# Pool sums moved from GpSimd to VectorE, one logarithm behind the last exponential, and the first gate matmuls between the last attention units of a fused decoder layer

## What is computed

```python
h = rms_norm(x, g_pre_mix); proj = h @ w_in            # q, k, v, u, gates
for window, dilation in ((128, 1), (512, 4), (2048, 16)):
    o_g, lse_g = dilated_window_attention(rope(q_g), rope(k_g), v_g)
o_attn = sum_g softmax_g(lse_g) * o_g                  # 4 heads x 64
y_pool = (trailing mean of u over 2/4/8/16 - u) @ w_pool_mix * pool_scale
merged = sigmoid(gate_a) * (o_attn @ w_proj_attn) + sigmoid(gate_p) * (y_pool @ w_proj_pool)
x = x + rms_norm(merged @ w_out, g_post_mix)
x = x + rms_norm(swiglu(rms_norm(x)) @ w_down)
```

## Time and profile before

| | us |
|---|---|
| runs | 996.31, 996.59, 1165.07; median 996.59 |
| profiled execution | 1000.57 |
| its span on the slowest core (core 7) | 999.0 |
| spans of the other cores | 989.2 to 997.9 |
| PE, DVE, ACT, POOL busy in the span | 926.5, 394.0, 350.3, 320.1 |
| attention stage on core 7 | 212.9 to 318.0 |

### The profile page before, as it was taken

How to read it: one execution, slowest core, us unless ns; L and a number is a source line. 1 busy time by engine, 2 the same in 40 slices (tenths; PEclk the granted TensorE clock), 3 DMA queues, 4 the chain that set the end, 5 groups by cost and what they waited for, 6 DMA issues and landing times.

```text
span 999.0 us, 15229 instructions; the slowest of 8 cores (989.2 to 999.0 us)
## 1 busy us (share of the span) xinstructions
PE 926.5 (93%) x5532; PEld 462.5 (46%) x5532; DVE 394.0 (39%) x552; ACT 350.3 (35%) x603; POOL 320.1 (32%) x318
## 2 busy tenths in 40 slices
PE   1779899998897999999998999999999999999993
PEld 1455454466664444444454444444444444444441
DVE  2576785558876233323677121111112111211111
ACT  4763763369776222224662111110111111111101
POOL 3446587733400433233565111111322000001231
PEclk9999999999998999999999999999999999999997
DMA  8799310000230452114979666664234444430332
GB/s 225 235 231 257 87 47 22 1 2 2 35 53 8 80 84 43 22 22 90 314 252 184 115 110 117 115 108 87 92 127 114 76 85 66 82 64 1 127 110 80
DMA packets 32874, 99.16 MB, mean 99 GB/s; under 512 B 4256, under 2 KB 4256, under 8 KB 32800
## 3 DMA queue, kind: packets, MB, share of 16 engines
q0 software_dynamic: 15296, 42.05, 25.7%
q1 hardware_dynamic: 17360, 56.11, 16.9%
q10 hardware_dynamic: 144, 0.03, 0.0%
HBM read 123.43 MB, written 16.78 MB: 140 GB/s over the span
## 4 chain that ended last, share of the span: by engine, by line
PE 80%; DMA 6%; ACT 4%; issue 4%; DVE 3%; POOL 2%; SPq 1%; DVEq 0%; ACTq 0%; POOLq 0%
PE ps L1229 15%; PE ps L1195 15%; PE ps L1198 15%; PE ps L449 10%; PE ps L969 6%; PE ps L972 6%; PE ps L538 5%; DMA xst<-xh 2%; DMA xin<-xo 2%; DMA xst<-xo 2%; PE ps L979 1%; PE ps L976 1%; PE ps L826 1%; PE ps L804 1%; POOL x1b L1045 1%
## 5 line engine op out<-in xcount | busy, mean ns | idle before, releaser
L1195 PE MATMUL ps<-hT,wgu 128*128 128x512 bf16 x672 | 158.7, 379 | 0.0
L1198 PE MATMUL ps<-hT,wgu 128*128 128x512 bf16 x672 | 158.7, 379 | 0.0
L1229 PE MATMUL ps<-wdn,ffT 128*128 128x512 bf16 x704 | 152.3, 379 | 1.5 <-DMA wdn<-wdn 1.5
L1210 DVE TENSOR_TENSOR ffT<-ps,sa 128x512 bf16<-128x512 f32 x88 | 60.8, 691 | 222.5 <-PE ps L1198 222.5
L1209 ACT ACTIVATE sa<-ps 128x512 f32<-128x512 f32 x88 | 52.7, 598 | 241.5 <-PE ps L1195 241.5
L1229 PEld LDWEIGHTS ps<-wdn,ffT 128*128 128x128 bf16 x704 | 68.8, 98 | 84.7 <-issue 1.9
L1198 PEld LDWEIGHTS ps<-hT,wgu 128*128 128x128 bf16 x672 | 65.7, 98 | 79.3
L1195 PEld LDWEIGHTS ps<-hT,wgu 128*128 128x128 bf16 x672 | 65.6, 98 | 78.6
L74 POOL DMA_DIRECT2D wgu<-wgu x42 | 22.5, 537 | 236.1 <-PE ps L1198 227.5
L449 PE MATMUL ps<-hT,wqk 128*128 128x512 bf16 x384 | 91.6, 383 | 0.6 <-DVE hT L432 0.6
L1045 POOL TENSOR_TENSOR x1b<-tb,xin 128x1024 f32<-128x1024 f32 x31 | 72.8, 2350 | 55.7 <-DVE tb L1040 29.9
(11 more groups left out here) (131 smaller groups left out, 1175.7 us busy)
## 6 DMA issues: line engine op xcount, KB each, us to landing
wgu<-wgu POOLq DMA_DIRECT2D x42, 512.0 KB, 6.3
xst<-xh SPq DMA_DIRECT2D x16, 512.0 KB, 16.7
xin<-xo SPq DMA_DIRECT2D x16, 512.0 KB, 5.4
x1s<-x1b SPq DMA_DIRECT2D x16, 512.0 KB, 3.7
xin<-x1s SPq DMA_DIRECT2D x16, 512.0 KB, 4.3
out<-x1b SPq DMA_DIRECT2D x15, 512.0 KB, 2.9
xst<-xo SPq DMA_DIRECT2D x12, 512.0 KB, 10.8
wdn<-wdn POOLq DMA_DIRECT2D x22, 256.0 KB, 7.3
```

The lines of the kernel that those rows point to most:

```text
L1195: e1 = pe.op(lambda e, k=k, wbuf=wbuf, ba=ba, tok=tok: e.matmul(ps[:, ba, :], lhsT=wbuf[:, 0, k, :], rhs=hT[:, k, tok], start=(k == 0), st ...
L1198: e2 = pe.op(lambda e, k=k, wbuf=wbuf, bb=bb, tok=tok: e.matmul(ps[:, bb, :], lhsT=wbuf[:, 1, k, :], rhs=hT[:, k, tok], start=(k == 0), st ...
L1210: ef = dve.op(lambda e, ub=ub, bb=bb, j=j, b=b: e.tensor_tensor(out=ffT[:, j, b * 512:(b + 1) * 512], in0=ps[:, bb, :], in1=sa[ub][:, :], ...
L1229: ev = pe.op(lambda e, j=j, h2=h2, pr_=pr_, il=il: e.matmul(ps[:, pr_[0] + h2, :], lhsT=ffT[:, j, il * 128:(il + 1) * 128], rhs=wdn[:, j, ...
```

## The change

It does four things. The adds of the second pool half run on DVE, in place of POOL, one in each of iterations 9 to 12, 17, 20, 23 and 26, with their means in 13, 14, 33 and 35; what depends on them moves too, the mapping to iterations 37 to 40 and the weight loads to 36. `norm_inv(2)` moves from iteration 46 to 47, behind the exponential of unit 47, and `norm_mul(2)` from 48 to 49. The 16 gate matmuls of the first merge unit are issued in iterations 45 to 49, ahead of the apply of that iteration, into banks 6 and 7, and the merge's bank sets become (6, 7, 0, 1) and (2, 3, 4, 5). The copy of unit 0 names its wait for the rotary stage itself.

```diff
-            ev2 = act.op(lambda e: e.activation(out=dst, in_=src, func=AF.Copy), waits=[ev])
+            ev2 = act.op(lambda e: e.activation(out=dst, in_=src, func=AF.Copy), waits=[ev] + (ev_rope if u == 0 else []))
...
-    h10, h11 = window_half(pool, 1, 0), window_half(pool, 1, 1)
+    h10, h11 = window_half(dve, 1, 0), window_half(dve, 1, 1)
+    c1_steps = dict(zip((9, 10, 11, 12, 13, 14, 17, 20, 23, 26, 33, 35), h10[0] + h10[1] + h11[0] + h11[1]))
...
+    def gate_mm():
+        n = len(ev_gate)
+        h, k, bank = n // 8, n % 8, 6 + n // 8
+        if k == 0:
+            pe.wait(bank_free[bank], wg_ev[0])
+        ev_gate.append(pe.op(lambda e: e.matmul(ps[:, bank, :], lhsT=wgs[0][:, h, k, :], rhs=hT[:, k, 0:512], start=(k == 0), stop=(k == 7)), signal=(k == 7)))
...
-        if 25 <= u < 29:
-            pool_mix(1, u - 25)
+        if u in c1_steps:
+            c1_steps[u]()
+        if 37 <= u < 41:
+            pool_mix(1, u - 37)
             ev_yp = act.last()
+        for _ in range({45: 3, 46: 3, 47: 3, 48: 4, 49: 3}.get(u, 0)):
+            gate_mm()
...
-        if u == 29:
+        if u == 36:
...
-        if u >= 38 and u % 4 == 2 and u < 50:
+        if u in (38, 42, 47):
             norm_inv((u - 38) // 4)
-        if u >= 40 and u % 4 == 0:
+        if u in (40, 44, 49):
             norm_mul((u - 40) // 4)
...
-    mring = Ring([(0, 1, 2, 3), (4, 5, 6, 7)])
+    mring = Ring([(6, 7, 0, 1), (2, 3, 4, 5)])
...
+            if mu == 1:
+                e1, e2 = ev_gate[7], ev_gate[15]
+            else:
```

More of the change, by code:

```diff
@@ L884, in build_program @@
     napp = 0
+    ev_gate = []
+    def gate_mm():
[4 more added lines that the diff above has]
+        ev_gate.append(pe.op(lambda e: e.matmul(ps[:, bank, :], lhsT=wgs[0][:, h, k, :], rhs=hT[:, k, 0:512], start=(k == 0), stop=(k == 7)), signal=(k == 7)))
     for u in range(-1, len(units) + 2):
@@ L899, in build_program @@
                 ev_z0.append(dve.last())
-                for f in h10[0]:
-                    f()
         if 12 <= u < 16:
             pool_mix(0, u - 12)
[L904 to L910, removed]
-        if 25 <= u < 29:
-            pool_mix(1, u - 25)
+        if u in c1_steps:
+            c1_steps[u]()
+        if 37 <= u < 41:
+            pool_mix(1, u - 37)
             ev_yp = act.last()
+        for _ in range({45: 3, 46: 3, 47: 3, 48: 4, 49: 3}.get(u, 0)):
+            gate_mm()
         if napp <= u - 2:
@@ L967, in build_program @@
             pe.wait(frm, bank_free[b1], bank_free[b2], bank_free[b3], bank_free[b4], ev_wg, ev_wp, ev_yp)
[L968 to L973, removed]
+            if mu == 1:
+                e1, e2 = ev_gate[7], ev_gate[15]
+            else:
+                for k in range(8):
+                    e1 = pe.op(lambda e, k=k, wb=wb, b1=b1, tok=tok: e.matmul(ps[:, b1, :], lhsT=wgs[wb][:, 0, k, :], rhs=hT[:, k, tok], start=(k == 0), stop=(k == 7)),
+                               signal=(k == 7))
+                for k in range(8):
+                    e2 = pe.op(lambda e, k=k, wb=wb, b2=b2, tok=tok: e.matmul(ps[:, b2, :], lhsT=wgs[wb][:, 1, k, :], rhs=hT[:, k, tok], start=(k == 0), stop=(k == 7)),
+                               signal=(k == 7))
             pe.wait(ev_oT[b])
```

## The result

The changed kernel takes 989.27 us (median of 6 runs, 988.52 to 990.98), beside 996.85 for the kernel before (median of 6). The ratio is 0.9927, 95% interval 0.9914 to 0.9941: 7.6 us in the median, under 1% and clearly more than nothing. The forecast was 989.6. The profiled execution took 988.52 us, where the forecast for it was 993.6; its slowest core (core 3) has a span of 987.0, the others 982.7 to 986.6.

The account below looks back on a forecast made before the run. TensorE was taken as the bound, with 14 idle microseconds in attention and slow matmuls around its end. 2.5 - 1.3 + 5.8 = 7.0 us won: 993.6 from the profiled 1000.57, 989.6 from the median 996.59; range 985.5 to 995.5.

Parts of the forecast that it names:

- First part: Attention stage, pool adds moved from POOL to DVE: 3.3 us of waits go, 0.8 come, 2.5 us won.
- allowed lateness: Units 17 to 26: spread adds may make DVE 1.7 us late before an apply waits; only the last two overstep.
- Second part: Pool maps and loads moved later: V block of unit 40 waits behind norm_inv(0) on ACT, 1.3 us lost.
- The weight loads are issued in unit 36 instead of 29.: Attention stage: loads land 9.0 us after issue, needed 17 us later; nothing lost, the 1.4 us V-block stop left.
- Third part, apply 47: Attention's end: norm_inv(2) behind exp 47 brings apply 47 to 315.0 instead of 316.99, 2.0 us won.
- Third part, apply 47 to the third merge unit: Merge start: 11.15 us becomes 7.35, 3.8 won with a new 1.4 us wait, half clock counted as gone.
- A microsecond won ahead of it should be a microsecond at the end.: Behind 318 us everything hangs on TensorE's own order, so attention-stage gains should reach the end whole.
- Rival 1: Clock falls anyway between units 45 and 49: 3.4 us of the gain lost, 993.0 us; chance 0.12.
- the early stretch: 235 to 248 us: clock stayed at 1.00 with TensorE busy 9.87 of 13.00 us, held against clock loss in gaps.
- Rival 2: DVE becomes the bound of units 17 to 35: 3.3 us lost instead of 0.8, 992.1 us; chance 0.12.
- Rival 3: Unit 40's 1.3 us stop lowers the clock until the merge: 7 us slower, 1003.6 us; chance 0.03.
- Rival 4: DVE and ACT hold the tail, apply 47 stays in place: 2.0 us less gain, 991.6 us; chance 0.10.

Follow-up runs that it names:

- gates back: Changed kernel with the 16 gate matmuls back behind the last apply, in the first merge unit: 993.06 us, ratio 0.9939 to the kernel before.
- sums back on POOL: Changed kernel with the second pool half's adds back on POOL and, with their means, at their old places: 993.40 us, ratio 0.9941 to the kernel before.
- logarithm at 47: Kernel before with only norm_inv(2) moved to iteration 47 and norm_mul(2) to 49: 996.92 us, ratio 0.9975 to the kernel before.
- no sums: Kernel before without the four POOL adds of the second pool half's second token half, means reading old sums: 999.67 us, timed once or twice.
- all three edits: Changed kernel with first logarithms at 40 and 43, second-token-half adds every fourth unit, last logarithm behind first merge sigmoids: 989.19 us; with banks renamed too, 988.97.
- logarithms at 40 and 43: Changed kernel with norm_inv(0) in iteration 40, norm_mul(0) in 42 and norm_inv(1) in 43: 991.99 us, timed once or twice.
- late loads: Kernel before with gate and mapping weight loads written in iteration 36, waiting for VectorE's last instruction there: 998.78 us, timed once or twice.

## Why the prediction was right

The stretch from the scores to the projection took 244.77 us on core 7 before and takes 237.86 on core 3 now, 6.9 us for the 7.0 of the sum. But that agreement is partly luck: two things that the prediction did not see, each of about 1.4 us, cancel on core 7 (a stop behind the weight loads that went away, and the projection that starts late). On the profiled execution the forecast missed: 993.6 against 988.52.

- **First part (2.5 expected).** Right in mechanism and size: 3.3 us of waits go and 1.0 comes (0.8 expected), 2.0 to 2.3 when taken back. The waits follow the second, third and fourth add, not only the last two: allowed lateness was put too high. The prediction gave the 3.3 to masks and means together; 2.3 of it goes when POOL's adds alone are left out.
- **Second part (1.3 lost).** The wait is 1.29 us, at the V block named. "1.3 us lost" was still too large as a term: removing it gains 0.35, since 0.9 comes back as waits of applies 44 and 45. The step that failed treats the terms of the second and third part as independent.
- **"The weight loads are issued in unit 36 instead of 29."** Wrong about the present: POOL's list is not tied to the loop on PE. The loads left when the mean they wait for was done, at 266.35 in the kernel before and at 287.01 now. And the stop that I "leave as it is" was tied to them: 0.2 to 1.4 us won on four cores.
- **Third part, apply 47 (2.0 expected).** Right: 2.2 with the logarithm alone on undisturbed cores, of which the gates in the gaps, which the sum took as free, cost up to 0.5 (99.26 against 98.74). From the scores to apply 47 the undisturbed cores go from 102.6 to 99.26, 3.3 us for 2.5 - 1.3 + 2.0 = 3.2.
- **Third part, apply 47 to the third merge unit (3.8 expected).** 318.35 - 310.74 = 7.61 us for 7.35, so 3.5 won, with a wait of 1.54 for 1.4. The clock stayed at 1.00, as counted.
- **"A microsecond won ahead of it should be a microsecond at the end."** This failed. From the third unit's gates to the projection it was 457.64 - 328.14 = 129.50 us and is 449.40 - 318.35 = 131.05. The new order of the bank sets costs 1.40 of the 1.55 at the other end of the merge, on all eight cores; I had read the line of the diff that does it for the start of the merge only. It failed the other way too: behind the projection's start the median of the cores is 538.1 to 538.3 us in the four kernels with the old bank sets and 535.9 to 537.1 in the ten profiles with the new ones, so the change seems to reach a part that the prediction took as untouched.
- **The rivals.** Rival 1 (clock falls anyway) did not come: from the scores to the projection the clock stayed at 1.00 on all cores of all eight kernels with gates in the gaps. The Trainium skill, page "TensorE: Matmul & The Clock Gate", section "A second HAM failure mode: psum-queue depth-cycling", tells of a clock that goes back and forth under short idles between groups of matmuls. These kernels, with waits of up to 1.64 us between groups, do not bear that out; but pauses without gates between them did lower the clock, on some cores and not on others, once even in the early stretch that the prediction held against the rule (gates back, core 0). Rival 2 (DVE becomes the bound) did not come: L735 starts at 262.19, before the mask of 261.59 + 0.71 ends, and the waits are 1.0 us. Its price was also too high: with four adds and not five its own figures give 4.0 - 1.7 = 2.3 us, not 3.3. Rival 3 (slower) had the clock fall behind unit 40; it did not. Rival 4 (apply 47 held) did not come either.
- **From the stretch to the median.** Of the median's 7.6 us, 6.2 lie in the stretch (medians over the cores), 0.8 short of the sum. The other 1.4 lies outside it. Part of that varies from execution to execution, but part comes with every kernel that has the new bank sets: behind the projection's start the cores of the changed kernel are 2.2 us shorter in the median (536.0 against 538.2), and the wait of 1.9 us for DVE's scaling, which four cores had, is gone. The core that set the profiled time had 541.36 us there before and 537.58 after. So the median of 989.27 for a forecast of 989.6 is in part luck too: 0.8 us less than expected inside the stretch, 1.4 us more outside it.

## What to carry to other kernels

When a ring of buffers or banks is turned to free some of them at the start of a loop, follow it to the loop's last turn: what the next stage takes first may now be what the loop gives back last. Two waits that lead to the same later instruction are not two terms of a sum; taking out the first shows how much of it the second takes back. A stop that disappears or appears at the border of two stages can change a wait far behind it, so compare what follows as well before you call it lost. A stage shorter by 4 us need not show in the time of the slowest core, when later stages differ by as much from core to core.

## What was not expected of the hardware

- The same program with the same pauses keeps TensorE's clock on some cores and loses it on others: with the gates back, seven cores fell to about half speed and one stayed at 1.00; with only the logarithm moved, six fell and two stayed. Behind apply 47 the loss was 0.9 to 2.2 us a core (for instance 239.02 against 240.03 in the stretch).
- Some 10 us behind two weight loads of 512 KB, TensorE stopped for 0.2 to 1.4 us, put down to an exponential, a mapping evacuation or to nothing. It hit three to five of eight cores (0.2 us or more) where the loads started at 261 to 267 us (the kernel before, sums back on POOL, logarithm at 47, no sums), four and three in the two kernels with all three edits and one with the logarithms at 40 and 43 (284 to 291 us), and none in the changed kernel or with late loads. That the loads are involved is shown by moving them alone, in one profiled execution; that the stop always stands at one of two places in TensorE's list is seen; by what way the loads stop TensorE is open.
- A VectorE wait in the second norm depends on what TensorE did 70 us earlier: 1.6 us or more on half of the cores where the output projection starts at once, never over 1.36 us where it starts 1.40 us late.
